# Expert values in two column halves, with seven products of block sums for eight block products in one of four weight slots

## The reference

```python
def peer_ffn(x, w_q, keys, u, v):       # 16384 experts, u and v are (16384, 2048)
    ...                                 # per token 8 heads choose 16 experts each: idx, gate
    ...                                 # y = sum over the chosen experts of
                                        #     gate * gelu(x . u[idx]) * v[idx]
    return y.reshape(B, S, D)

        x = x + peer_ffn(rmsnorm_2(x, norm2_w[l]), peer_w_q[l], peer_keys[l], peer_u[l], peer_v[l])
    return rmsnorm_2(x, final_norm_w)
```

## Time and profile before

| | us |
|---|---|
| median of 3 runs | 2844.89 (2844.86 to 2845.9) |
| the profiled execution | 2844.47 |
| its span, first to last instruction | 2842.6 |
| PE busy / DVE / ACT / POOL | 2821.8 / 1862.1 / 1258.5 / 703.4 |
| stage of the expert values on PE | from 2134.7 to 2831.5 |

### The profile page before, as it was taken

How to read it: one execution, slowest core, us unless ns; L and a number is a source line. 1 busy time by engine, 2 the same in 40 slices (tenths; PEclk the granted TensorE clock), 3 DMA queues, 4 the chain that set the end, 5 groups by cost and what they waited for, 6 DMA issues and landing times.

```text
span 2842.6 us, 40357 instructions
## 1 busy us (share of the span) xinstructions
PE 2821.8 (99%) x15369; PEld 2450.3 (86%) x15369; DVE 1862.1 (66%) x2529; ACT 1258.5 (44%) x1407; POOL 703.4 (25%) x454
## 2 busy tenths in 40 slices
PE   9999999999999999999999999999999999999998
PEld 8888888999988889878888888888888888888886
DVE  5657777665665666775899996555655555555555
ACT  4336644544345444554444443433434444444444
POOL 0000025222000000000387877888730000000000
PEclk9999999999999999999999999999999999999999
DMA  6556645667555554444577777666666666666665
GB/s 230 193 199 239 220 149 174 202 215 237 197 188 184 188 205 161 153 153 182 172 209 210 208 214 217 195 185 188 192 203 237 241 242 241 232 216 216 216 216 190
DMA packets 153185, 576.22 MB, mean 203 GB/s; under 512 B 50688, under 2 KB 83584, under 8 KB 90496
## 3 DMA queue, kind: packets, MB, share of 16 engines
q1 hardware_dynamic: 71136, 513.95, 51.5%
q10 hardware_dynamic: 38944, 44.06, 4.5%
q0 software_dynamic: 43008, 16.93, 3.6%
HBM read 547.47 MB, written 27.39 MB: 202 GB/s over the span
## 4 chain that ended last, share of the span: by engine, by line
PE 97%; DVE 2%; ACT 1%; issue 0%; DMA 0%; ACTq 0%; SPq 0%; DVEq 0%
PE bank L551 34%; PE bank L1125 24%; PE bank L556 18%; PE bank L647 11%; PE bank L537 2%; PE bank L878 2%; PE bank L834 1%; DVE wlo L1896 1%; PE bank L743 1%; PE bank L901 1%; PE bank L819 0%; PE bank L722 0%; PE bank L805 0%; PE bank L806 0%; ACT whi L1160 0%
## 5 line engine op out<-in xcount | busy, mean ns | idle before, releaser
L1896 DVE TENSOR_TENSOR wlo<-raw,whi 128x2048 fp32r<-128x2048 f32 (+1 forms) x481 | 1097.4, 2282 | 759.5 <-ACT whi L1160 756.8
L1160 ACT ACTIVATE whi<-raw 128x2048 fp32r<-128x2048 f32 (+1 forms) x483 | 919.9, 1905 | 1309.9 <-PE bank L551 684.7
L551 PE MATMUL bank<-hT,whi 128*128 128x512 f32 x3776 | 924.9, 393 | 0.0
L551 PEld LDWEIGHTS bank<-hT,whi 128*128 128x128 f32 x3776 | 690.6, 188 | 129.3 <-issue 0.2
L1858 POOL DMA_INDIRECT gates_dram<-R x256 | 580.8, 2269 | 264.4 <-DVE R L2728 145.2
L556 PEld LDWEIGHTS bank<-hT,wlo 128*128 128x128 f32 x3776 | 483.9, 191 | 18.7
L556 PE MATMUL bank<-hT,wlo 128*128 128x256 f32 x3776 | 489.5, 283 | 0.0
L1125 PE MATMUL bank<-whi,ghi 128*128 128x512 f32 x1016 | 271.8, 389 | 0.2 <-issue 0.2
L1125 PE MATMUL bank<-wlo,ghi 128*128 128x512 f32 x1016 | 271.6, 389 | 0.0
L1125 PE MATMUL bank<-whi,glo 128*128 128x512 f32 x1016 | 271.5, 389 | 0.0
L647 PE MATMUL bank<-whi,hT 128*128 128x512 f32 x1016 | 244.1, 392 | 2.8 <-DVE hT L1886 1.7
(11 more groups left out here) (381 smaller groups left out, 2238.4 us busy)
## 6 DMA issues: line engine op xcount, KB each, us to landing
raw<-stream SPq DMA_DIRECT2D x483, 1024.0 KB, 4.8
gates_dram<-token_scale POOLq DMA_DIRECT2D x128, 128.0 KB, 4.8
R<-gates_dram ACTq DMA_DIRECT2D x128, 128.0 KB, 3.9
R<-cmpw ACTq DMA_DIRECT2D x16, 512.0 KB, 4.8
acts_dram<-R ACTq DMA_DIRECT2D x32, 256.0 KB, 5.4
R<-acts_dram ACTq DMA_DIRECT2D x64, 128.0 KB, 3.8
gates_dram<-R POOLq DMA_INDIRECT x256
xres<-x SPq DMA_DIRECT2D x2, 1024.0 KB, 6.1
```

The costliest lines, as they stand in the source:

```text
L551: return mm(bank[to][:], whi[t][:, k * P:(k + 1) * P], h[:, k, :, :].rearrange("p a t -> p (a t)"), start=(at == 0), stop=(at == KC - 1))
L1160: A(whi[t][:, 0:w], raw[t][:, 0:w], ACT.Copy).then_inc(hi_ready[t], 1)
L1896: V.tensor_tensor(wlo[t][:, 0:w], raw[t][:, 0:w], whi[t][:, 0:w].bitcast(F32), ALU.subtract).then_inc(raw_free[t], 1)
```

## The change

The values are stored on the host in another order. A slot now holds 256 experts (two blocks of 128, `e` = 0, 1) and 1024 columns (two pieces of 512, `d` = 0, 1). The first 64 slots, groups 0 to 15, hold the first 1024 columns of all experts, the last 64 the other half. A plain slot still has 24 matmuls: four outputs (token block, column piece) in banks 4 to 7, two expert blocks, three products. The banks are read and started anew at the middle.

Each slot needs the activations of two blocks, so tiles of gates and activations are 256 KB, and since each half goes over all experts, activations are loaded and multiplied twice for groups 0 to 7 and 16 to 23. In groups 8 to 15 the product is written over `late`, and groups 24 to 31 take it from there with no loading and no product. The product moves from VectorE to GpSimd. `low_acts` and its rounding now work on 128x512 and stand, on VectorE, ahead of the low part of the weights.

Slot 1 of each group is a 2x2 by 2x2 product of blocks (token blocks and expert blocks, expert blocks and column pieces), and is done with seven products in Winograd's form: GpSimd makes four differences of weight blocks `T1` to `T4` from `raw[1]` (`block_sums`), VectorE four sums of activation blocks (`sum_blocks`), and both are split into high and low parts like everything else (`high_blocks`, `high_sums` on ScalarE, `low_blocks`, `low_sums` on VectorE). Seven products of three matmuls are 21. Three of them add to the plain banks, four to banks 0 to 3. At the end of a half VectorE combines banks 0 to 3 into the residual (`join`), and adds the plain banks (`add_plain`). The space of `t_sum`, `t_hi`, `t_lo` is that of `hT2`, which is free in this stage. To find semaphores for this, some are merged.

```diff
-            def expert_values(i, first, slots=RING):
-            ...
+            def plain_values(i, s, first=False, again=False, last=False):
+                t = s % 2
+                pe.wait_ge(hi_ready[t], v_high(i, s))
+                pe.wait_ge(acts_split[t], acts(i, s))
+                ...
+                for q in range(4):
+                    if again:
+                        pe.wait_ge(x3_ready, q + 1)
+                    for n, x_ in enumerate((gh, gl)):
+                        for e in range(2):
+                            product(x_, whi, e, q, start=((first or again) and n == 0 and e == 0), stop=False)
+                ...
+                pe.wait_ge(raw_free[t], consumed("peer_v", i, s))
+                for q in range(4):
+                    for e in range(2):
+                        done = product(gh, wlo, e, q, start=False, stop=False)
+                done.then_inc(slot_used[t], 1)
+            def joined_values(i, first=False, again=False, last=False):
+                ...
+                pe.wait_ge(hi_ready[1], v_high(i, 1))
+                pe.wait_ge(acts_split[1], acts(i, 1))
+                ...
+                for to, x_, at in raws[0:2]:
+                    for h in range(2):
+                        mm(bank[to][:], x_(h), whi[1][:, block_of(*at)], start=(new and h == 0 and to == m1), stop=False)
+                pe.wait_ge(acts_split[1], acts(i, 1, 1))
+                ...
+                for n, (to, x_, at) in enumerate(sums_):
+                    if n % 2 == 0:
+                        pe.wait_ge(hi_ready[1], v_high(i, 1, n // 2 + 1))
+                    for h in range(2):
+                        mm(bank[to][:], x_(h), t_hi[:, at, :], start=(new and h == 0 and to != c21), stop=False)
+                pe.wait_ge(raw_free[1], consumed("peer_v", i, 1))
+                for to, x_, at in raws:
+                    mm(bank[to][:], x_(0), wlo[1][:, block_of(*at)], start=False, stop=(last and to == m1))
+                for to, x_, at in sums_:
+                    done = mm(bank[to][:], x_(0), t_lo[:, at, :], start=False, stop=(last and to != c21))
+                done.then_inc(slot_used[1], 1)
 # ScalarE
+            def value_slot(i, s, kept, load=None):
+                split("peer_v", i, s)
+                high_acts(i, s, kept)
+                if s == 1:
+                    high_blocks(i, 0)
+                    high_sums(i)
+                    high_blocks(i, 1)
+                if load is not None:
+                    next_tile(i, s, *load)
 # GpSimd
+            def product(i, s, kept, reuse=True):
+                t = s % 2
+                pool.wait_ge(gate_tile_in[s], i * 16 + 16)
+                src = values_of(i, s, kept)
+                if kept is None:
+                    pool.wait_ge(act_tile_in[s], (i * 16 + 16) if reuse != "again" else (i * 16 - 112))
+                    if reuse:
+                        pool.wait_ge(acts_split[t], acts(i, s - 2, 1 if s == 3 else 0) if s >= 2 else acts(i - 1, s + 2))
+                    nc.gpsimd.tensor_tensor(src, gate_tile[:, s, :, :], act_tile[:, s, :, :], ALU.mult).then_inc(product_made, 1)
+                else:
+                    nc.gpsimd.tensor_tensor(src, gate_tile[:, s, :, :], src, ALU.mult).then_inc(product_made, 1)
+            def block_sums(i):
+                r = raw[1]
+                pool.wait_ge(slot_full[1], loaded("peer_v", i, 1))
+                ...
+                TT = nc.gpsimd.tensor_tensor
+                TT(t_sum[:, T1, :], r[:, block_of(0, 1)], r[:, block_of(0, 0)], ALU.subtract).then_inc(t_summed, 1)
+                TT(t_sum[:, T3, :], r[:, block_of(1, 1)], r[:, block_of(0, 1)], ALU.subtract).then_inc(t_summed, 1)
+                pool.wait_ge(t_summed, i * 4 + 2)
+                TT(t_sum[:, T2, :], r[:, block_of(1, 1)], t_sum[:, T1, :], ALU.subtract).then_inc(t_summed, 1)
+                pool.wait_ge(t_summed, i * 4 + 3)
+                TT(t_sum[:, T4, :], r[:, block_of(1, 0)], t_sum[:, T2, :], ALU.subtract).then_inc(t_summed, 1)
+            def value_slots(i, kept, reuse=True):
+                for s in (1, 2, 3):
+                    if kept != 1 and not (s == 1 and reuse is False):
+                        product(i, s, kept, reuse)
+                    if s == 1:
+                        block_sums(i)
 # VectorE
-            def product(i, s, src, at):
-            ...
+            def low_blocks(i, half):
+                at = slice(2 * half, 2 * half + 2)
+                dve.wait_ge(hi_ready[1], v_high(i, 1, half + 1))
+                last = V.tensor_tensor(t_lo[:, at, :], t_sum[:, at, :], t_hi[:, at, :].bitcast(F32), ALU.subtract)
+                if half == 1:
+                    last.then_inc(raw_free[1], 1)
+            def low_weights(i, s):
+                t = s % 2
+                dve.wait_ge(hi_ready[t], v_high(i, s))
+                last = V.tensor_tensor(wlo[t][:], raw[t][:], whi[t][:].bitcast(F32), ALU.subtract)
+                if s != 1:
+                    last.then_inc(raw_free[t], 1)
+            def value_slot(i, s, kept):
+                if s == 1:
+                    sum_blocks(i, kept)
+                low_acts(i, s, kept)
+                low_weights(i, s)
+                if s == 1:
+                    low_blocks(i, 0)
+                    low_sums(i)
+                    low_blocks(i, 1)
+            def join(p):
+                ...
+                V.tensor_tensor(x11, m1, x11, ALU.add)
+                step(V.tensor_copy(u, m1))
+                step(V.tensor_tensor(u, m6, u, ALU.add))
+                step(V.tensor_tensor(v, m5, u, ALU.add))
+                step(V.tensor_tensor(u, m7, u, ALU.add))
+                V.tensor_tensor(x12, x12, v, ALU.add)
+                V.tensor_tensor(x21, x21, u, ALU.add)
+                step(V.tensor_tensor(x22, x22, u, ALU.add))
+                V.tensor_tensor(x22, m5, x22, ALU.add).then_inc(sums_read, 1)
+            with dve.Fori(8, 16) as i:
+                value_slots(i, 0)
+            join(0)
+            low_acts(16, 0, None)
+            add_plain(0)
+            low_weights(16, 0)
 # host
-    peer_v = i["peer_v_2"][0].reshape(NK, P, SLOT)
+    peer_v = i["peer_v_2"][0].reshape(NK // 2, 2, P, 2, CW).transpose(3, 0, 2, 1, 4).reshape(NK, P, SLOT)
```

More of the change, by code:

```diff
@@ L1148, in _ @@
+            with pe.Fori(n // 2 + 1, n - 1) as i:
+                value_group(i)
+            value_group(n - 1, last=True)
         @block.scalar
@@ L1763, in _ @@
             for s in range(2):
                 high_acts(0, s)
-                next_tile(0, s, True)
+                next_tile(0, s, 0)
             split("peer_v", 0, 1)
             gelu_pair(NK // 2 - 1)
+            high_blocks(0, 0)
+            high_sums(0)
+            high_blocks(0, 1)
             for s in range(2, RING):
-                split("peer_v", 0, s)
-                high_acts(0, s)
-                next_tile(0, s, True)
-            with act.Fori(1, n // 2 - 1) as i:
-                for s in range(RING):
-                    split("peer_v", i, s)
-                    high_acts(i, s)
-                    next_tile(i, s, True)
@@ new lines, in _ @@
+            value_slots(15, 0, [GATES] + [BOTH_AGAIN] * 3)
+            value_slots(16, None, [BOTH_AGAIN] * 4)
+            for at in range(4):
+                square_x3(at)
+            with act.Fori(17, 23) as i:
+                value_slots(i, None, [BOTH_AGAIN] * 4)
+            value_slots(23, None, [BOTH_AGAIN] + [None] * 3)
+            with act.Fori(24, 32) as i:
+                value_slots(i, 1, [None] * 4)
+            A(rt, msq, ACT.Sqrt)
+            for at in range(4, 8):
+                square_x3(at)
@@ L1870, in _ @@
+            value_slots(23, None, "again")
+            with pool.Fori(24, 32) as i:
+                value_slots(i, 1)
+            pool.wait_ge(fnw_in, 16)
+            pool.wait_ge(x3_ready, 4)
+            for b in (1, 0):
+                for c in range(2):
+                    cs = slice(c * 512, (c + 1) * 512)
+                    nc.gpsimd.tensor_tensor(weighted[:, b, cs], xres[:, b, cs], raw[0][:, cs], ALU.mult).then_inc(x3_weighted[b], 1)
         @block.vector
@@ L2319, in restore_x2 @@
                     last = V.tensor_scalar(xres[:, b, :], scr_of[1][:, b * D:(b + 1) * D], scales[:, b:b + 1], None, ALU.mult)
-                last.then_inc(x2_back, 1)
+                step(last)
             def evac_scaled(n):
@@ L2780, in _ @@
                 choose(*part_of(2 * PH + slot))
-            n = G0["peer_v"][1]
-            for s in range(2):
-                product(0, s, act_tile, s)
-            for s in range(2):
-                low_acts(0, s)
+            low_acts(0, 0, None)
+            sum_blocks(0, None)
+            low_acts(0, 1, None)
             sum_acts(NK - 1)
             scale_acts()
-            product(0, 2, act_tile, 2)
-            split("peer_v", 0, 1)
+            low_weights(0, 1)
+            low_blocks(0, 0)
@@ L2791, in _ @@
```

(33 more changed lines are left out.)

308 lines of the change are left out of this document (186 added, 122 removed).

## The result

| | before | after |
|---|---|---|
| median, us | 2844.88 | 3064.68 (4 runs, 3059.2 to 3071.3) |
| ratio, 95% interval | | 1.0774 [1.0761, 1.0788] |
| profiled execution, us / its span | 2844.47 / 2842.6 | 3071.32 / 3069.5 |
| mean granted clock of TensorE | 0.999 | 0.972 |
| expert values, us for a group of four slots | 21.8 | 27.3 to 30.7 |

What follows compares the result with a forecast made beforehand. TensorE, 99% busy, was taken to bound the kernel before. 2844.5 + 206 (raw[1]'s cycle with VectorE and GpSimd taking turns) + 20 (clock) + 10 (join) = 3080.5, say 3080 us; range 2910 to 3160.

Steps and rivals of the forecast that it cites:

- That TensorE stops being last, and that raw[1] is late: Expert values: weight buffer raw[1], shared by slots 1 and 3, sets the pace; TensorE falls from 99% to some 75% busy.
- The ring, 24.3 us: raw[1] in a group: slot 1's legs 8.65, slot 3's 5.52, two loads at 5.1 us; 81 us over all groups.
- no exclusion: Rival: VectorE and GpSimd do not block each other on these shapes, raw[1]'s cycle alone costs; 2936 us, chance 14%.
- Exclusion: VectorE and GpSimd take turns on SBUF inputs, adding GpSimd operations of 1.29 us to raw[1]'s cycle; +206 us in all.
- The layout of slot 1: Slot 1's operations laid out one at a time from raw[1]'s landing: low_sums ends at 11.5 us, second low_blocks at 12.7.
- The clock, +20: TensorE's 6.9 us gap in slot 1 can lower its granted clock; +20 us, between bounds 0 and 51.
- The join, +10: VectorE's `join`, in the middle and at the end of the value stage, and once-only work; +10 us, bounds 3 to 20.
- Tile loads at nothing: The 256 KB gate and activation tile loads cost nothing; raw loads stay at 4.8 us.
- loads that collide: Rival: every raw load takes 6.3 us beside tile loads of twice the size; +96, 3176 us, chance 8%.
- Spacing unchanged at 0.2268: TensorE's expert-value matmuls priced at 0.2268 us each; 96 removed ones take 21.8 us off TensorE.
- TensorE stays last: Rival: raw[1]'s cycle closes within 21.1 us, so TensorE sets the group's time; 2829 us, chance 7%.
- Sum: Whole kernel: 2844.5 + 206 + 20 + 10 = 3080.5, say 3080 us.

Runs made afterwards that it cites:

- e11: The changed kernel with `gh` and `gl` placed where `hT` lay and the differences in their place; 3065.97 us, 1.0785.
- e5: The changed kernel with twelve multiplications by zero per group on TensorE, ahead of its wait in slot 1; 3054.61 us, 1.0741.
- e1: The changed kernel with GpSimd's products and differences cut to 8 columns of each block behind group 0, every wait kept; 2941.84 us, 1.0335.
- e2: The changed kernel with only GpSimd's four block differences cut to 8 columns behind group 0, products whole; 2967.67 us, 1.0429.
- e4: The changed kernel with slot 1 plain too: 24 matmuls in every slot, no differences, sums or join; 2868.56 us, 1.0080.
- e9: The changed kernel with products and differences on VectorE, `gh` and `gl` where `hT` lay, sums of activations rounded in slot 0; 2909.19 us, 1.0228.
- e8: The changed kernel with all slots plain (24 matmuls, no differences, sums or join), and `gh` and `gl` where `hT` lay; 2859.82 us, 1.0050.

## Why the prediction was right

**That TensorE stops being last, and that raw[1] is late:** right in the main. Slot 3's `whi` waits for its load in 24 of 32 groups, as forecast; slot 1's does in only 11, and in 20 TensorE still releases it, up to 1.0 us late. e11 shows that the end does not follow TensorE's spacing, e5 that its clock still counts for a little.

**The ring, 24.3 us:** right in size. With GpSimd out of the way (e1) groups without both kinds of tile take 24.0 and 24.1 us. The rival "no exclusion" at 2936 is nearly what e1 measured, 2941.8, so it was the right price for a case that did not occur, though not from the same parts: the ring came out some 10 us under its 81, and the tile loads below are in the 2941.8.

**Exclusion:** the mechanism is right; by e1 it is worth 122.8 us, the clock's part included, where the forecast's terms without the clock and the join (206 - 81) give 125. That the two are so close is in part luck, as the parts were off in opposite ways. Differences: forecast 2 x 1.29 x 32 = 83, measured 97.0. Products: forecast 32 x 1.29 = 41, measured 25.8, nothing in groups 0 to 7 and 3.4 us a group in 8 to 15 instead of 2.6. The layout of slot 1 had left out the four sums of 128x128, and they are what the differences meet in groups 24 to 31: with all four stretched to 1.2 to 1.4 us there, the second `low_blocks` ends 11.2 to 11.7 us after the start of T1, for 8.1 to 8.7 in e2, though `wlo` takes its 2.28. The 26.9 us forecast for these groups, from T2 and T4 behind `low_acts` and `wlo`, came near the 27.3 by another leg.

The Trainium skill, "SBUF — State Buffer", section "Who interferes with whom", says of the exclusive lock that the order of issue, not the shape, decides who blocks. The timeline agrees both ways: T2, issued before `wlo`, ended first and `wlo` took 3.39 us; T4, issued during `wlo`, ended behind it and took 3.19.

**The layout of slot 1:** forecast `low_sums` to end 11.5 us and the second `low_blocks` 12.7 us after landing; in the group shown `glo` ends at 10.3 (2285.77) and TensorE waits 4.35 us, not 6.9, since TensorE itself arrives late (6.0 us after landing and not 4.6). The second `low_blocks` ends at 11.5 (2286.91 by the trace).

**The clock, +20:** the direction is right, the size twice what e5 gave back (10.1). But e5 left a third of the slow matmuls, so the whole price is not known. The upper bound had 3.9 us of slowing in slot 1; the group shown has 2.9, the median group, with 7 slow spacings, some 1.4. What TensorE adds to the ring of raw[1] is small: it releases slot 1's `whi` in 20 groups and slot 3's in 8, up to 1.0 us after the landing, some 16 us in all.

**The join, +10:** by the starts of T1, groups 16 and 17 take 30.6 and 31.3 us and the next two 27.6 and 28.1: some 6 us in the middle. Not all of it is the join: in group 17 two loads of raw[1] take 5.9 and 7.1 us for a median of 4.8. In e1 the second `low_blocks` of group 16 ends 12.1 us after the start of T1, for 8.1 to 8.9 in the groups around it, which makes some 4 us. What the end adds was not taken apart.

**Tile loads at nothing:** a step that failed, by e1. Its groups with both kinds of tile take 25.1 us (without group 0, which keeps the whole operations, and group 16, which has the join) against 24.0 in the others, which is 1.1 x 16, some 18 us. The earlier trace rows showed a median of 4.8, and a median hides the few loads of up to 7.9 on which a ring without slack has to wait. That the tile loads are the cause is read from where the long loads lie; no run took them away. It is a fifth of the rival "loads that collide" (96), and stayed hidden in the sum because the join and the bare ring (24.0 for 24.3) came out lower.

**Spacing unchanged at 0.2268:** wrong, 0.2325 to 0.2329 as placed. It did not show in the time, because TensorE was not last. In e4, where TensorE is last, it costs 18 us, most of the 21.8 that the removed matmuls were to bring. So the rival "TensorE stays last" at 2829 would have been too low by that.

**Sum:** forecast 206 + 20 + 10; the group starts give 8 x (28.1 + 30.7 + 29.0) + 8 x 27.3 = 920.8, +224 over 696.7, with the clock and the join inside. They are of the profiled execution, which is 226.9 us above the one before; the medians differ by 219.8.

## What to carry to other kernels

Before work is given to an idle GpSimd, look at what runs on VectorE at that moment: where both read two tensors from SBUF they take turns, and 10 us of "free" work a group cost more than on the busy engine. When an operation is moved ahead in one queue, look for what stands behind it there (e9), and count the ring of a buffer by its slowest loads, not by their median. Where the matmul's spacing is the whole price, measure it with the operands where they will lie.

## What the runs showed of the hardware that was not expected

- The spacing of 128x512 fp32r matmuls depends on where the block held still lies in SBUF: 0.2329 us at one place, 0.2263 at another (e4, e8), with order, banks and operand shapes equal. No run here tells why.
- VectorE and GpSimd in steady alternation: a 128x128 sum of 0.28 us takes up to 1.40, GpSimd's 128x512 product of 1.29 up to 3.3.
- In one group a wait of 4.35 us put TensorE at 0.427 us a matmul for the next 5.7 us; in the same group of e5, twelve multiplications by zero in the gap, with 3.06 us of idle time left behind them, kept it at 0.23. In other groups of e5 slow matmuls are left.
